# A fused decoder step on Trainium2: the output projection with the merged rows stationary and 512 output columns moving, and three staging buffers for the merge's gate tiles

## What is computed

```python
def _merge(x, o_fox, fg, o_gla, gg, ma, mb, gla_norm_g, w_up_a, w_up_b, w_out):
    B, L, _ = x.shape
    a = (o_fox.reshape(B, L, FOX_WIDTH) * jax.nn.silu(fg)) @ w_up_a
    o_gla = _rmsnorm(o_gla, gla_norm_g).reshape(B, L, GLA_VW)
    b = (o_gla * jax.nn.silu(gg)) @ w_up_b
    m = jax.nn.sigmoid(ma) * a + jax.nn.sigmoid(mb) * b
    return x + m @ w_out
```

## Time and profile before

| what | value |
|---|---|
| median of three runs | 1675.98 us (1675.61 to 1684.03) |
| the profiled execution | 1682.01 us |
| its span | 1680.2 us |
| mean granted TensorE clock | 0.976 of full |
| PE busy | 1548.9 us (92%) |
| DVE, ACT, POOL busy | 671.7, 614.6, 501.6 us |

### The profile page before, as it was taken

One profiled execution on the slowest core, in us unless ns is written; L12 is line 12 of the kernel. 1 busy time (PEld: TensorE's weight loads), 2 busy tenths in 40 slices (PEclk: granted clock), 3 DMA queues, 4 the chain that ended last, 5 costly groups with the idle time before them and its releaser, 6 DMA issues.

```text
span 1680.2 us, 34414 instructions
## 1 busy us (share of the span) xinstructions
PE 1548.9 (92%) x11497; PEld 1290.4 (77%) x11497; DVE 671.7 (40%) x1504; ACT 614.6 (37%) x1311; POOL 501.6 (30%) x952
## 2 busy tenths in 40 slices
PE   6989998998799998999999999999998868999997
PEld 5878787776687876787877877778766767888987
DVE  4444343635344444534446344553443122233111
ACT  5344434444433434334444334433433243111111
POOL 3444344420090233432453332542330122111000
PEclk9999999998999999999999999999999889999999
DMA  4121212120165576776767676777656463322243
GB/s 166 31 82 43 67 43 81 56 77 28 53 207 172 166 228 181 240 229 185 242 215 253 213 216 202 223 235 227 191 170 204 132 216 101 118 97 71 79 117 93
DMA packets 156831, 250.00 MB, mean 149 GB/s; under 512 B 37449, under 2 KB 65610, under 8 KB 156146
## 3 DMA queue, kind: packets, MB, share of 16 engines
q1 hardware_dynamic: 125074, 215.78, 41.0%
q0 software_dynamic: 31584, 32.02, 6.3%
HBM read 217.47 MB, written 30.22 MB: 147 GB/s over the span
## 4 chain that ended last, share of the span: by engine, by line
PE 59%; ACT 3%; DVE 3%; DMA 3%; issue 2%; SPq 1%; POOL 0%; DVEq 0%; ACTq 0%
PE psum L284 29%; PE psum L1891 7%; PE psum L2341 6%; PE psum L1906 4%; PE psum L2333 4%; PE psum L1939 3%; DMA tmp_gates<-con 2%; PE psum L2012 1%; PE psum L2022 1%; DMA v_page<-in_cache_v 1%; PE psum L2019 1%; PE psum L1982 1%; PE psum L1922 1%; DVE w_lo L259 1%; PE psum L2030 1%
## 5 line engine op out<-in xcount | busy, mean ns | idle before, releaser
L284 PE MATMUL psum<-h_hi,w_hi 128*128 128x384 f32 (+1 forms) x1536 | 561.4, 365 | 38.1 <-DVEq L2278 15.0
L284 PE MATMUL psum<-h_hi,w_lo 128*128 128x384 f32 (+1 forms) x1536 | 511.6, 333 | 0.0
L284 PE MATMUL psum<-h_lo,w_hi 128*128 128x384 f32 (+1 forms) x1536 | 510.5, 332 | 0.0
L284 PEld LDWEIGHTS psum<-h_hi,w_hi 128*128 128x128 f32 x1536 | 295.7, 193 | 121.0 <-issue 107.0
L1461 POOL DMA_DIRECT2D sc<-tmp_bias x512 | 252.6, 502 | 308.9 <-PE psum L1922 306.0
L284 PEld LDWEIGHTS psum<-h_lo,w_hi 128*128 128x128 f32 x1536 | 296.6, 193 | 2.6 <-issue 0.3
L284 PEld LDWEIGHTS psum<-h_hi,w_lo 128*128 128x128 f32 x1536 | 295.0, 192 | 0.0
L670 POOL DMA_DIRECT2D lfp<-in_cache_logf x256 | 124.1, 485 | 178.1 <-issue 178.1
L1891 PE MATMUL psum<-con,k_page 128*128 128x128 f32 x1024 | 152.5, 276 | 9.6 <-DVE k_t L1391 6.3
L1510 ACT ACTIVATE k_t<-psum 128x512 f32<-128x512 f32 x128 | 76.1, 595 | 186.9 <-PE psum L1891 186.9
L1891 PEld LDWEIGHTS psum<-con,k_page 128*128 128x128 f32 x1024 | 120.9, 141 | 30.3 <-issue 26.2
(11 more groups left out here) (237 smaller groups left out, 1950.4 us busy)
## 6 DMA issues: line engine op xcount, KB each, us to landing
k_page<-in_cache_k SPq DMA_DIRECT2D x256, 256.0 KB, 3.5
v_page<-in_cache_v SPq DMA_DIRECT2D x256, 256.0 KB, 3.1
w_raw<-in_w_tiles SPq DMA_DIRECT2D x63, 512.0 KB, 4.6
g_pair<-tmp_gates SPq DMA_DIRECT2D x16, 544.0 KB, 4.6
sc<-tmp_bias POOLq DMA_DIRECT2D x512, 16.0 KB, 2.9
tmp_ogla<-gate POOLq DMA_DIRECT2D x4, 1088.0 KB, 5.9
g_pair<-tmp_ogla SPq DMA_DIRECT2D x8, 544.0 KB, 5.3
x_in<-in_x_prompt SPq DMA_DIRECT2D x8, 512.0 KB, 6.5
```

Source lines behind the costliest of these rows:

```text
L284: m = pe.matmul(out, wt[:, s, k, :], h[:, k, t0:t0 + w], start=(k == 0 and a == 0), stop=(k == KT_ - 1 and a == 2))
```

## The change

**Gate staging.** `tm` becomes three tiles of 384 columns of `con` (columns 128 to 1280), used by chunk number modulo three. Each has its own store semaphore, and ACT waits only for the store of three chunks before. The tiles now reach into the scan masks, so the stage waits for the last scan (`dc_cum`) too.

**Output.** The operands change places: `m` (128 features x 128 rows, `h_hi` or `h_lo`) is stationary and 512 output columns of the weights move. A bank then holds 128 rows x 512 output columns already row-major, so `y_fm`, the transposes and ACT's copies go away. The output is done in two halves of 512 columns. In a half, the eight banks gather the eight row tiles of the prompt over all 8 feature tiles; a weight tile j now covers 2 feature tiles x 512 output columns (4 tiles for a half), read from memory in pieces of 256 elements. Each of the eight split tiles has its own place (`wo_hi`, `wo_lo` for tiles 2 to 7), so the splits are not held back by PE. The x rows are loaded straight into `y_tok`, and DVE adds into it. The 64 sample rows come last, in banks 0 and 1.

```diff
+        w_out = ins["w_tiles"][4 * NHP + 6 * GH + 2 * KT_:4 * NHP + 6 * GH + 3 * KT_]
+        for half in range(2):
+            sources += [w_out[4 * half:4 * half + 4, :, 2 * k:2 * k + 2, :].rearrange("j p k c -> p j k c") for k in range(KT_ // 2)]
...
+            dst = self.raw[:] if len(src.shape) == 3 else self.raw[:].rearrange("p (j k) c -> p j k c", k=2)
+            sp.dma_start(dst, src).then_inc(self.loaded, 16)
...
+            W(eng, "dc_cum", GH - 1, 3)
...
+        wo_hi = sb(ctx, "wo_hi", [P, KT_ - 2, KT_, P], F32R)
+        wo_lo = sb(ctx, "wo_lo", [P, KT_ - 2, KT_, P], F32R)
+        y_tok = sb(ctx, "y_tok", [P, 2, TT, 512])
+        y_smp = sb(ctx, "y_smp", [NSAMP, 2, 512])
+        tm = [con[:, P + 384 * s:P + 384 * (s + 1)] for s in range(3)]
...
+            wait_up_done(sp)
+            x_load(0)
+            for j in range(KT_ - 2):
+                stream.load(sp, OUT + j)
+                if j == 1:
+                    x_load(1)
+                    for half in range(2):
+                        sp.dma_start(y_smp[:, half, :], xs[:, half * 512:(half + 1) * 512]).then_inc(xs_in, 16)
+            for half in range(2):
+                for t in range(TT):
+                    W(sp, "y_set", half, t + 1)
+                    sp.dma_start(yp[t * P:(t + 1) * P, half * 512:(half + 1) * 512], y_tok[:, half, t, :]).then_inc(y_out, 16)
...
-                    if n or c:
-                        act.wait_ge(m_out, 16 * (3 * n + c))
+                    if n:
+                        act.wait_ge(m_out[c], 16 * n)
...
+            wait_up_done(act)
+            for j in range(1, KT_):
+                k = base + OUT + j
+                act.wait_ge(stream.loaded, 16 * k)
+                act.activation(wo(j)[0], stream.raw[:], ACT.Copy).then_inc(stream.hi_set, 1)
...
+            for j in range(1, KT_):
+                k = base + OUT + j
+                hi, lo = wo(j)
+                dve.wait_ge(stream.hi_set, 1 + k + 1)
+                dve.tensor_tensor(lo, stream.raw[:], hi.bitcast(F32), ALU.subtract).then_inc(stream.lo_set, 1)
+            for half in range(2):
+                dve.wait_ge(x_in[half], 16 * TT)
+                for t in range(TT):
+                    W(dve, "y_mm", half, t + 1)
+                    y = y_tok[:, half, t, :]
+                    inc(dve.tensor_tensor(y, bank[t], y, ALU.add), "y_set")
...
+            for half in range(2):
+                for j in range(4 * half, 4 * half + 4):
+                    pe.wait_ge(stream.lo_set, 1 + base + OUT + j + 1)
+                    for kk in range(2):
+                        first_k, last_k = j % 4 + kk == 0, j % 4 == 3 and kk == 1
+                        if last_k and half == 0:
+                            pe.wait_ge(m_lo_end, 3)
+                        for t in range(TT):
+                            if first_k and half:
+                                W(pe, "y_set", 0, t + 1)
...
+                            for a, (v, w) in enumerate(terms(j, kk, slice(t * P, (t + 1) * P))):
+                                m = pe.matmul(bank[t].rearrange("p (j c) -> p j c", c=P), v, w, start=(first_k and a == 0), stop=(last_k and a == 2))
...
+            W(pe, "y_set", 1, 2)
+            for j in range(4):
+                for kk in range(2):
+                    for a in range(3):
+                        for half in range(2):
+                            v, w = terms(4 * half + j, kk, slice(SEQ, NT))[a]
+                            m = pe.matmul(bank[half][0:NSAMP, :].rearrange("p (j c) -> p j c", c=P), v, w, start=(j + kk + a == 0), stop=(j == 3 and kk == 1 and a == 2))
```

More of the change, by code:

```diff
@@ L2121, in build_merge @@
         x_in = [sem(f"xr_in{s}") for s in range(2)]
-        y_out = [sem(f"y_out{s}") for s in range(2)]
+        y_out, xs_in, smp_mm, smp_set = sem("y_out"), sem("xs_in"), sem("smp_mm"), sem("smp_set")
         base = 4 * NHP + 6 * GH + first
@@ L2136, in inc, with wo, wait_up_done @@
             m.then_inc(S[name], 1)
+        def wo(j):
+            if j < 2:
+                return stream.hi[:, (base + OUT + j) % 2], stream.lo[:, (base + OUT + j) % 2]
+            return wo_hi[:, j - 2], wo_lo[:, j - 2]
+        def wait_up_done(eng):
+            eng.wait_ge(stream.projected, stream.chunk(OUT - 1, 2))
         def wait_ol(eng, k):
@@ L2162, in g_load @@
                 if 2 * j == first:
-                    sp.wait_ge(m_out, 3 * NG * 16)
+                    for s in range(3):
+                        sp.wait_ge(m_out[s], NG * 16)
                 for x in range(2):
                     sp.dma_start(g[:, 2 * (j % 2) + x, :], gates[2 * j + x]).then_inc(g_in[j % 2], 16)
[L2167 to L2172, removed]
             stream.load(sp, 0)
@@ L2221, in _ @@
                     W(pool, "m_sig", n, c + 1)
-                    pool.dma_start(gates[first + n, :, t0:t0 + w], tm[:, 0:w]).then_inc(m_out, 16)
+                    x = 3 * n + c
+                    pool.dma_start(gates[first + n, :, t0:t0 + w], tm[x % 3][:, 0:w]).then_inc(m_out[x % 3], 16)
             for j in range(KT_ - 1):
@@ L2227, in _ @@
                                            stream.h_hi[:, j, t0:t0 + w].bitcast(F32), ALU.subtract), "m_lo")
-            pool.wait_ge(m_out, 3 * NG * 16)
+            for s in range(3):
+                pool.wait_ge(m_out[s], NG * 16)
         @block.scalar
@@ L2297, in _ @@
                                           ALU.subtract).then_inc(m_lo_end, 1)
[L2298 to L2313, removed]
+            wait_up_done(dve)
+            for j in range(1, KT_):
[9 more added lines that the diff above has]
+                    inc(dve.tensor_tensor(y, bank[t], y, ALU.add), "y_set")
+            dve.wait_ge(xs_in, 32)
+            dve.wait_ge(smp_mm, 2)
+            for half in range(2):
+                m = dve.tensor_tensor(y_smp[:, half, :], bank[half][0:NSAMP, :], y_smp[:, half, :], ALU.add)
+            m.then_inc(smp_set, 1)
         @block.tensor
         def _(pe):
-            opened(pe, *(S[n] for n in ("a_mm", "y_turned")))
+            opened(pe, *(S[n] for n in ("a_mm", "y_mm")))
             for n in range(NG):
@@ L2343, in _ @@
                     m.then_inc(stream.projected, 1)
[L2345 to L2357, removed]
             for j in range(KT_ - 1):
@@ L2361, in _, with terms @@
             pe.wait_ge(S["m_lo"], 3 * (KT_ - 1))
[L2362 to L2371, removed]
+            def terms(j, kk, rows):
+                hi, lo = wo(j)
+                k = 2 * (j % 4) + kk
+                m_hi, m_lo = stream.h_hi[:, k, rows], stream.h_lo[:, k, rows]
+                return [(v, w.rearrange("p (j k) c -> p k j c", k=2)[:, kk]) for v, w in ((m_hi, hi), (m_hi, lo), (m_lo, hi))]
@@ new lines, in _ @@
+            for half in range(2):
+                for j in range(4 * half, 4 * half + 4):
[4 more added lines that the diff above has]
+                            pe.wait_ge(m_lo_end, 3)
+                        for t in range(TT):
+                            if first_k and half:
+                                W(pe, "y_set", 0, t + 1)
+                            if first_k and not half and 2 <= t < 5:
+                                W(pe, "a_read", KT_ - 1, t - 1)
+                            if first_k and not half and t >= 5:
+                                pe.wait_ge(stream.z_read, stream.chunk(OUT - 1, t - 5))
+                            for a, (v, w) in enumerate(terms(j, kk, slice(t * P, (t + 1) * P))):
+                                m = pe.matmul(bank[t].rearrange("p (j c) -> p j c", c=P), v, w, start=(first_k and a == 0), stop=(last_k and a == 2))
+                            if last_k:
+                                inc(m, "y_mm")
@@ new lines, in _ @@
+            W(pe, "y_set", 1, 2)
+            for j in range(4):
+                for kk in range(2):
+                    for a in range(3):
+                        for half in range(2):
+                            v, w = terms(4 * half + j, kk, slice(SEQ, NT))[a]
+                            m = pe.matmul(bank[half][0:NSAMP, :].rearrange("p (j c) -> p j c", c=P), v, w, start=(j + kk + a == 0), stop=(j == 3 and kk == 1 and a == 2))
+                            if j == 3 and kk == 1 and a == 2:
+                                m.then_inc(smp_mm, 1)
```

44 lines of the change are left out of this document (11 added, 33 removed).

## The result

The change is faster by 1.7%, which is less than forecast, and its median lies above the range of 1627 to 1649. Six executions have a median of 1651.35 us (1644.44 to 1653.76). Of the kernel before there are six as well, with a median of 1680.46 us, and one of them, at 2497.35 us, is left out of the ratio. The ratio to it is 0.9832, with a 95% interval of 0.9803 to 0.9861. In a later timing it was 0.9807 (0.9784 to 0.9831).

A forecast was written before the change was run, and what follows sets the result against it. It took the single staging tile's store wait to bound the gate stage, and transposes and waits to lengthen the output loop. 25.7 + 15.2 = 40.9 us, taken from the median 1675.98, gave 1635 us, range 1627 to 1649.

The forecast's parts named there:

- half clock: Start of the up stage: matmuls at the 1.2 GHz level behind an idle PE, 3.1 us that should go.
- The cost of the matmuls: Output stage: 432 matmuls of 512 columns at 0.228 us, 43.8 us a half, samples 10.9, together 98.5 us.
- rival (e): Output matmuls: PE reads the four-piece moving operand at half rate, stage 92 us longer, 1727 us; chance 0.03.
- when tile 7 is split: Output stage: DVE splits the last weight tile at +43.4 us, just before PE leaves half 0 at +43.8.
- The photo finish: Boundary of the output halves: tile 7's split nearly ties with PE's end of half 0; stall 0.3 us, pacing 0.3.
- rival (b): Output boundary: tile 7 late at about +49.5, PE stands some 6 us, half clock 3.1 more, 1644 us; chance 0.25.
- an estimate of 21 us a block: Output stage's x loads: eight 256 KB transfers without overlap at 2.6 us each, putting tile 7 near +70.
- The gate stage's replay: Gate stage: PE and ACT replayed from rows, up stage starting at 1380.0 instead of 1402.65, 22.6 us gained.
- rival (c): Gate stage: ACT falls behind after a late reload, gain 13 us instead of 25.7, 1648 us; chance 0.1.
- The level: Whole kernel: starting time for the subtraction, 1675.98 us, the median of three executions.

The follow-up runs named there:

- the parts: The kernel before with the three staging buffers alone: 24 us less than before; the change with a single staging buffer, as before: 10 us less than before.
- Adds first: The change with DVE's split of the last weight tile moved behind the adds of the first half; 1639.70 us, ratio to before 0.9775.
- Gates only: The kernel before with the three staging buffers alone; 1656.29 us, ratio to before 0.9857.
- FoX late: The change with loads of the FoX output and first two up_a tiles issued behind the last reload of o; 1649.93 us, ratio to before 0.9817.
- FoX behind weight: The all three kernel with the FoX loads one place later, behind the load of the first w_up_b tile; 1639.98 us, ratio to before 0.9752.
- all three: The change with the edits of Adds first, x late and FoX late together; 1640.24 us, ratio to before 0.9777.
- x late: The change with the second x block and the samples' x issued behind the last weight load; 1641.70 us, ratio to before 0.9766.

## Why the prediction was wrong

**The direction and the two mechanisms were right.** The store wait was the gate stage's bound, the transposed loop the output stage's; the parts gave 24 and 10 us. The up stage lost its half clock, 2.8 us against 3.1 forecast. That it began at 1379.0 us, next to the 1380.0 of the forecast, is luck: the gate stage was 3.4 us longer than forecast and began 4.4 us earlier.

**The cost of the matmuls was right.** Half 0 takes 43.7 us from its first matmul's start to its last one's end (43.8 forecast), the samples 11.06 (10.9), the tail 6.1 with the adds (6.9). The spacing in it is 0.227 us on average, that of the line through the two shorter forms. The 216 ns of the Trainium skill ("TensorE: Matmul & The Clock Gate", "Back-to-back issue gap") is 11 ns too short here, as at 384 columns. Reading the moving operand in four pieces cost nothing, so rival (e) is out.

**The step that failed first: when tile 7 is split.** The prediction put it at +43.4; it came at +47.0. Tiles 2 and 4 were split 1.7 and 4.2 us later than their forecast marks of +11.5 and +25.4; the plain rounds behind them took 5.8 us where 6.0 were forecast. I had charged a queue of x by its bytes at 375 GB/s and one fixed latency; for tiles 2 and 4 that was 5.1 and 5.5 us from issue to landing, and they took 6.8 and 8.1. The page "DMA: Bandwidth & Descriptors", section "Issuing engines are not separate DMA queues", of the Trainium skill says that all transfers interleave on the same 16 engines; the rows agree, a tile of the usual 3.4 us took 8.1 beside 2.4 MB. The photo finish was lost by 3.9 us, and the half clock behind the 4.2 us pause cost 1.7 more. That was rival (b), at a lower price: 5.6 us more than the forecast instead of 8.5. Adds first shows that this was more than the whole of the output stage's miss of 4.3 us; without it the stage is 104.2 us, 1.8 under the forecast. The fixed 2.0 us for each transfer, from which the prediction made an estimate of 21 us a block, are given in the section "Anatomy of one DMA" of the Trainium skill for transfers issued by GpSimd; those here are issued by SP, and the first block with tile 2 behind it had landed 10.8 us after its first issue.

**The gate stage's replay** was 3.4 us too short, 44.2 against 47.6. Its sum has ACT's work, one reload of o and PE's matmuls, and no wait for a weight tile at all. In the trace of before the tile for chunk 9 was issued late, at 1367.1, and landed in 4.5 us. With faster chunks SP issued it at 1351.8, into the tail of the FoX loads, and it took 9.0 us. PE paused 2.0 us and ran 3.2 us at the half clock. Gates only, with 7.6 us of landing, came to 44.9, and FoX late as well: the replay itself was sound, and rival (c), ACT as the bound, wrong: in FoX behind weight PE's matmuls alone fill the chain, and the stage takes 43.6 us.

**The level.** I subtracted from 1675.98, the median of three. Seventeen later executions of the kernel before ran from 1671.59 to 1686.01 with a median of 1680.57. Their time follows their mean clock, 0.983 at the fastest, 0.974 at the slowest. The level was 4.5 us too low. With 33.0 us from 1680.5 the sum is 1647.5, inside the range; the measured 1651.35 is 3.9 us above that, 1648.55 of the second timing 1.1. What set apart the executions of one program ahead of the merge was not tried. In all, the 16.4 us between 1635 and 1651.35 are 7.9 in the stages (3.4 gates, 4.3 output, 0.2 up), 4.5 in the level, and 3.9 whose cause stays open. None of the three alone would have put the time above the range.

## What to carry to other kernels

When operands change places, the matmul time follows from the spacing of the forms in the trace; what has to be worked out with care is which engine's order now puts the freeing of a buffer behind a late arrival. Where a forecast ends in a tie between two engines, price the loser's wait and the clock behind it, and take the tie out by moving one line. A large load needed later should not be issued in front of a small one that is needed at once, and moving it means looking at the next small one too. And when executions of a kernel differ by more than the terms of the sum, compare stages between common events rather than whole times.

## What I had not expected of the hardware

An idle PE of 2.0 us (gates of the change) and of 2.24 us (all three) was followed by the 1.2 GHz level, one of 1.7 us (adds first, x late) was not, nor one of 2.04 us in the gate stage of before; so the length alone does not decide. Nor did the half clock always come at once: in the gates of the change PE had run 1.2 us at full rate again, and 1.0 us behind the pause at 1580, but behind the pauses of 4.8 and 5.1 us at the same place in FoX late and in the second trace of the change the first matmul already took 0.76 and 0.77 us, against 0.47 behind the 4.2 us of the first trace.

A transfer of 512 KB cut into pieces of 1 KB landed in 3.4 us with nothing else on the way, no later than one in pieces of 4 KB (3.5 to 4.3 us in the trace of before, some of them beside loads of x and stores).
